# Sliding attention: the second product with the values stationary and the probabilities moving

## The reference, cut to what matters

```
sc = einsum('bcqhgd,bckhd->bchgqk', qb, kb) * HEAD_DIM ** -0.5      # kb, vb: the chunk before and the own chunk
sc = where(mask, sc, NEG_INF)
probs = softmax(concatenate([sc, sink], -1))[..., :-1]
o = einsum('bchgqk,bckhd->bcqhgd', probs, vb)                        # then reshape to (b, s, C_WIDTH)
mix = concatenate([y_a, y_b, y_c], -1) @ w_out[i]
```

## Time and profile before

| | |
|---|---|
| three runs, median (lowest to highest) | 1235.37 us (1234.68 to 1235.66) |
| profiled execution, span | 1233.0 us |
| its own time | not listed apart from the three runs |
| TensorE busy | 1226.3 us, 99% |
| VectorE busy | 839.8 us, 68% |
| ScalarE busy | 610.8 us, 50% |
| GpSimd busy | 136.2 us, 11% |
| TensorE's granted clock | 1.000 on average |

### The profile page before, as it was taken

How to read it: one execution, slowest core, us unless ns; L and a number is a source line. 1 busy time by engine, 2 the same in 40 slices (tenths; PEclk the granted TensorE clock), 3 DMA queues, 4 the chain that set the end, 5 groups by cost and what they waited for, 6 DMA issues and landing times.

```text
span 1233.0 us, 20630 instructions
## 1 busy us (share of the span) xinstructions
PE 1226.3 (99%) x8009; PEld 1128.1 (91%) x8009; DVE 839.8 (68%) x1365; ACT 610.8 (50%) x1156; POOL 136.2 (11%) x209
## 2 busy tenths in 40 slices
PE   9999999999999999999999999999999999999998
PEld 8999888999999998888899999889999999888887
DVE  5675545988888853268976746368888887433788
ACT  7444334555555642237664444264655555322474
POOL 2003531000000000003030036120000000000120
PEclk9999999999999999999999999999999999999999
DMA  7323232233333353320242222322333333444001
GB/s 251 104 65 90 70 103 69 69 102 105 104 103 103 103 188 142 131 69 18 86 122 68 90 65 69 103 77 67 114 104 103 104 103 121 154 154 171 18 18 69
DMA packets 124464, 122.32 MB, mean 99 GB/s; under 512 B 5200, under 2 KB 108752, under 8 KB 124368
## 3 DMA queue, kind: packets, MB, share of 16 engines
q1 hardware_dynamic: 123680, 120.48, 31.0%
q10 hardware_dynamic: 688, 0.53, 0.1%
HBM read 118.90 MB, written 2.10 MB: 98 GB/s over the span
## 4 chain that ended last, share of the span: by engine, by line
PE 98%; DVE 1%; ACT 0%; POOL 0%; issue 0%; DVEq 0%; ACTq 0%
PE bank L993 30%; PE bank L995 30%; PE bank L994 30%; PE bank L1203 2%; PE bank L1262 1%; PE bank L1285 1%; PE bank L1331 1%; PE bank L1283 1%; PE bank L1315 1%; PE bank L1270 0%; PE bank L1307 0%; PE bank L1327 0%; PE bank L1336 0%; PE bank L1213 0%; PE bank L1357 0%; PE bank L1244 0%
## 5 line engine op out<-in xcount | busy, mean ns | idle before, releaser
L993 PE MATMUL bank<-w_hi,h_hi 128*128 128x384 f32 (+2 forms) x564 | 201.2, 357 | 0.6 <-DVE w_lo L1892 0.5
L994 PE MATMUL bank<-w_lo,h_hi 128*128 128x384 f32 (+2 forms) x564 | 194.7, 345 | 0.0
L1890 DVE TENSOR_TENSOR w_lo<-raw,w_hi 128x1024 fp32r<-128x1024 f32 x70 | 83.7, 1234 | 133.7 <-ACT w_hi L1409 133.4
L993 PE MATMUL bank<-h_hi,w_hi 128*128 128x256 f32 x568 | 161.0, 284 | 0.1
L995 PE MATMUL bank<-h_hi,w_lo 128*128 128x256 f32 x568 | 160.7, 283 | 0.0
L994 PE MATMUL bank<-h_lo,w_hi 128*128 128x256 f32 x568 | 160.7, 283 | 0.0
L995 PE MATMUL bank<-w_hi,h_lo 128*128 128x384 f32 (+2 forms) x468 | 157.5, 337 | 0.0
L1409 ACT ACTIVATE w_hi<-raw 128x1024 fp32r<-128x1024 f32 x70 | 70.6, 1053 | 160.6 <-PE bank L995 160.6
L995 PE MATMUL bank<-w_hi,mid_lo 128*128 128x512 f32 x352 | 137.0, 389 | 0.0
L993 PE MATMUL bank<-T_hi,w_hi 128*128 128x256 f32 x448 | 126.8, 283 | 0.0
L994 PE MATMUL bank<-T_lo,w_hi 128*128 128x256 f32 x448 | 126.8, 283 | 0.0
(11 more groups left out here) (296 smaller groups left out, 2942.8 us busy)
## 6 DMA issues: line engine op xcount, KB each, us to landing
raw<-in_w_ffn_in SPq DMA_DIRECT2D x88, 512.0 KB, 3.9
raw<-in_w_ffn_out SPq DMA_DIRECT2D x44, 512.0 KB, 4.2
raw<-in_w_in SPq DMA_DIRECT2D x40, 384.0 KB, 3.8
raw<-in_w_out SPq DMA_DIRECT2D x16, 512.0 KB, 3.8
gw<-in_w_gate SPq DMA_DIRECT2D x16, 512.0 KB, 3.7
raw<-in_w_in SPq DMA_DIRECT2D x10, 512.0 KB, 4.1
raw<-in_w_ple SPq DMA_DIRECT2D x4, 512.0 KB, 6.3
x<-in_x_in SPq DMA_DIRECT2D x3, 512.0 KB, 6.9
```

Source lines behind the costliest of these rows:

```text
L993: pe.matmul(out_ap, a_hi, b_hi, start=start, stop=False, skip_group_check=True)
L994: pe.matmul(out_ap, a_hi, b_lo, start=False, stop=False, skip_group_check=True)
L1890: last = dve.tensor_tensor(lo, raw[q % RAWS][:, cols], hi, ALU.subtract)
```

## The change

The second product is turned round. Stationary are now the values (128 keys by 64 values of one group), moving are the transposed probabilities of the three heads of the group (384 columns). The result stands transposed in PSUM, group 0 on partitions 0 to 63 and group 1 on 64 to 127, so the transposes of `swa_yT` and their step are gone, and `y_hi` and `y_lo` are made at `swa_o`. As no ones column can give the sums any more, the exponentials write them (`accum_out`), and the probabilities are scaled before they are transposed, in a new step `swa_norm` on VectorE at u+4. The transposes move to u+5 and the product to u+7. The two heads that now share a row of 128 are one of each group, so the rows of `w_out` are put in that order before the launch.

```diff
-        for step, name in zip((0, 1, 4, 6, 8), ("swa_cur", "swa_prev", "swa_PT", "swa_o", "swa_yT")):
+        for step, name in zip((0, 1, 4, 5, 7), ("swa_cur", "swa_prev", "swa_norm", "swa_PT", "swa_o")):
...
-    swa_y = [place(f"swa_y{i}", [P, C_HEADS, HD], F32, (110, 48)[i]) for i in range(2)]
...
-    cv = place("cv", [P, TILES, 2, HD + 1], F32, 207.75)
-    dv = place("dv", [P, 2, 2, HD + 1], F32, 210)
+    cv = place("cv", [P, TILES, 2, HD], F32, 207.75)
+    dv = place("dv", [P, 2, 2, HD], F32, 210)
...
                 elif kind == "swa_PT":
                     c = e[1]
-                    pe.wait_ge(swa_exp, layer * TILES + c + 1)
+                    pe.wait_ge(swa_pn, layer * TILES + c + 1)
...
-                    for hh in range(C_HEADS):
-                        o = swa_bank(c, 0)[:, hh * (HD + 1):(hh + 1) * (HD + 1)]
-                        g = hh // 3
-                        if c:
-                            pe.matmul(o, ptu[c % 2][:, hh, :], cv[:, c - 1, g, :], start=True, stop=False,
-                                      skip_group_check=True)
-                        last = pe.matmul(o, ptl[c % 2][:, hh, :], dv[:, c % 2, g, :] if c else cv[:, 0, g, :],
-                                         start=(c == 0), stop=True, skip_group_check=True)
-                    last.then_inc(swa_o, 1)
-                elif kind == "swa_yT":
-                    c = e[1]
-                    pe.wait_ge(swa_yr, layer * TILES + c + 1)
-                    flat = swa_y[c % 2][:, :, :].rearrange("p h d -> p (h d)")
-                    for k in range(3):
-                        last = pe.transpose(swa_bank(c, 1)[:, k * P:(k + 1) * P], flat[:, k * P:(k + 1) * P],
-                                            T_("ident"))
+                    pairs = ([(ptu[c % 2], cv[:, c - 1, :, :]), (ptl[c % 2], dv[:, c % 2, :, :])] if c
+                             else [(ptl[0], cv[:, 0, :, :])])
+                    for i, (probs, values) in enumerate(pairs):
+                        for g in range(2):
+                            last = pe.matmul(swa_bank(c, 1)[rows(g), 0:BW], values[:, g, :],
+                                             probs[:, 3 * g:3 * g + 3, :], start=(i == 0),
+                                             stop=(i == len(pairs) - 1), skip_group_check=True)
                     last.then_inc(y_T, 1)
...
                     if c >= 2:
-                        act.wait_ge(y_T, y_count(layer, ("swa_yT", c - 2)))
+                        act.wait_ge(swa_PT, layer * TILES + c - 1)
...
                         act.activation(prob[c % 2][:, hh, :], prob[c % 2][:, hh, :], ACT.Exp, scale=HD ** -0.5,
-                                       bias=negm[c % 2][:, hh:hh + 1])
+                                       bias=negm[c % 2][:, hh:hh + 1], accum_out=psum_k[c % 2][:, hh:hh + 1])
...
                     if c > 2:
-                        pool.wait_ge(swa_o, layer * TILES + c - 1)
+                        pool.wait_ge(y_T, y_count(layer, ("swa_o", c - 2)))
...
+                elif kind == "swa_norm":
+                    c = e[1]
+                    o = c % 2
+                    dve.wait_ge(swa_exp, layer * TILES + c + 1)
+                    step(dve.tensor_tensor(rl[o], psum_k[o], esink[o], ALU.add))
+                    step(dve.reciprocal(rl[o], rl[o]))
+                    done(dve.tensor_tensor(prob[o][:], prob[o][:], rl[o][:, :, None].to_broadcast([P, 6, P]),
+                                           ALU.mult), swa_pn)
...
                 elif kind == "swa_o":
-                    c = e[1]
-                    o = c % 2
-                    dve.wait_ge(swa_exp, layer * TILES + c + 1)
-                    dve.wait_ge(swa_o, layer * TILES + c + 1)
-                    both = swa_bank(c, 0)[:, 0:6 * (HD + 1)].rearrange("p (h e) -> p h e", h=6)
-                    step(dve.tensor_tensor(rl[o], both[:, :, HD], esink[o], ALU.add))
-                    step(dve.reciprocal(rl[o], rl[o]))
-                    done(dve.tensor_tensor(swa_y[o][:], both[:, :, 0:HD],
-                                           rl[o][:, :, None].to_broadcast([P, 6, HD]), ALU.mult), swa_yr)
-                elif kind == "swa_yT":
                     c = e[1]
                     y_split(layer, e, swa_bank(c, 1)[:, 0:BW].rearrange("p (k t) -> p k t", k=3),
                             y_hi[:, 5:8, c * P:(c + 1) * P], y_lo[:, 5:8, c * P:(c + 1) * P])
...
+def heads_in_pairs(w):
+
+    low = AW + BW
+    c = w[:, low:].reshape(w.shape[0], C_KV, C_HEADS // C_KV, HD, D).transpose(0, 2, 1, 3, 4)
+    return np.concatenate([w[:, :low], c.reshape(w.shape[0], C_HEADS * HD, D)], 1)
```

More of the change, by code:

```diff
@@ L33 @@
 C_HEADS = 6
+C_KV = 2
 BW = B_HEADS * HD
@@ L514, in build_trunk @@
     esink = [small(6) for _ in range(2)]
+    psum_k = [small(6) for _ in range(2)]
     rl = [small(6) for _ in range(2)]
@@ L587, in build_trunk @@
     dv_ready = sem("dv_ready")
-    swa_o = sem("swa_o")
-    swa_yr = sem("swa_yr")
+    swa_pn = sem("swa_pn")
     ret_T = sem("ret_T")
@@ L665, in build_trunk @@
     for layer, e in schedule:
-        if e[0] in ("swa_yT", "ret_yT", "gmlp_yT"):
+        if e[0] in ("swa_o", "ret_yT", "gmlp_yT"):
             order_yT += [(layer, e)] * (2 if e[0] == "gmlp_yT" else 1)
@@ L1158, in block_of @@
                             pe.wait_ge(y_lo_ready, y_count(layer, ("ret_yT", 3)))
-                    need = {2: ("ret_yT", m), 3: ("swa_yT", m), 1: ("ret_yT", m), 0: ("gmlp_yT",)}[i]
+                    need = {2: ("ret_yT", m), 3: ("swa_o", m), 1: ("ret_yT", m), 0: ("gmlp_yT",)}[i]
                     if m == 3:
@@ L1255, in _ @@
                         if c >= 2:
-                            pe.wait_ge(y_lo_ready, y_count(layer, ("swa_yT", c - 2)))
+                            pe.wait_ge(y_lo_ready, y_count(layer, ("swa_o", c - 2)))
                     else:
@@ L1302, in _ @@
                     else:
-                        pe.wait_ge(y_lo_ready, y_count(layer, ("swa_yT", 2)))
+                        pe.wait_ge(y_lo_ready, y_count(layer, ("swa_o", 2)))
                     for i, src in enumerate((bk, bq)):
@@ L1343, in _ @@
                     if c == 0:
-                        pe.wait_ge(y_lo_ready, y_count(layer, ("swa_yT", 3)))
+                        pe.wait_ge(y_lo_ready, y_count(layer, ("swa_o", 3)))
                     elif c < TILES - 1:
@@ L1690, in _ @@
                                    ACT.Copy).then_inc(pt_copied0, 1)
-                elif kind == "swa_yT":
+                elif kind == "swa_o":
                     c = e[1]
@@ L1759, in _ @@
             pool.memset(neg_big, NEG).then_inc(pool_init, 1)
-            pool.memset(cv[:, :, :, HD:HD + 1], 1.0).then_inc(pool_init, 1)
-            pool.wait_ge(pool_init, 3)
+            pool.wait_ge(pool_init, 2)
             def pre(layer, stage, m):
@@ L1945, in _ @@
             dve.memset(still[:], 0.0).then_inc(still_zero, 1)
-            dve.wait_ge(pool_init, 3)
+            dve.wait_ge(pool_init, 2)
             spent = {}
@@ L2387 @@
         "bs_t": np.asarray(gmlp_bs).transpose(0, 2, 1),
-        "gn_w": np.asarray(ret_gn_w).reshape(depth, 3, P).transpose(0, 2, 1), "sinks": attn_sinks, "w_out": w_out, "post_mix": norm_mix_post,
+        "gn_w": np.asarray(ret_gn_w).reshape(depth, 3, P).transpose(0, 2, 1), "sinks": attn_sinks, "w_out": heads_in_pairs(np.asarray(w_out)), "post_mix": norm_mix_post,
         "w_ffn_in": w_ffn_in, "w_ffn_out": w_ffn_out, "post_ffn": norm_ffn_post,
```

## The result

The changed kernel takes 1250.39 us (median of 4 runs, 1249.01 to 1252.59), the kernel before 1235.24 us beside it. The ratio is 1.0125, with a 95% interval from 1.0112 to 1.0138: 15.2 us slower, where 12.0 were forecast. Slower, inside the range of 1240 to 1253, and 3.0 us above the predicted 1247.4. The share lost is small, but clear of the interval. Its four runs go from 1249.0 us at a mean granted clock of 0.996 to 1252.6 at 0.992.

The account below looks back on a forecast made before the run. TensorE was taken to bound the kernel, busy 1226.3 of 1233.0 us. Per layer, 9.7 us of waits against 3.7 saved gave 6.0, so +12.0 on the median 1235.37: 1247.4 us, range 1240 to 1253.

Parts of the forecast that it names:

- The mechanism: Before the probability transposes in attention: TensorE waits for VectorE's late scaling, 9.7 us of waits a layer.
- Waits in layer 0: TensorE before the transposes of chunks 0 to 3: 3.2, 1.0, 2.9 and 1.9 us.
- VectorE's signal of chunk 0: End of chunk 0's scaling at 59.7 us, with TensorE ready for the transposes at 56.55 us.
- The saving: TensorE's own attention work: 10.7 us removed and 6.95 added, so 3.7 us less a layer.
- the new product: Turned second product on TensorE: 1.9 us a chunk with change of shape, 1.25 in chunk 0.
- The 0.322 us for an instruction: New product on TensorE: each 384-column f32 instruction, scaled by columns from 0.215 for the gMLP product's 256.
- The factor of 0.68: New product's two column halves side by side on TensorE: time multiplied by 0.68, eight instructions in 1.75 us.
- The score product: Nearest row for overlapping halves on TensorE: 0.073 us per 128-column instruction where half of 0.215 would be 0.107.
- Rival 2: Same waits, but TensorE's clock falls after chunks 0 and 2 of both layers, 2 to 4 us each: 1253 to 1260; chance 0.12.
- The wait of chunk 3's scores: TensorE waits 0.7 us for ScalarE's late score copies, behind the 512-column split between norm and chunk 2's mask.
- The sums: On ScalarE, accumulator reads behind the six exponentials: 0.09 us each, 0.55 a chunk.
- The other side: Rival 3: VectorE keeps up, waits stay below 3.7 us a layer, faster, 1228.0 us with none; chance 0.08.

Follow-up runs that it names:

- e1: Changed kernel without the scaling of the probabilities and TensorE's wait for it (sum and reciprocal stay, output not normalized): 1233.1 us.
- e5: Changed kernel without the scaling (output not normalized), transposes and product back at their old places u+4 and u+6: 1226.5 us.
- e2: Changed kernel with the scaling at unit u+2 in place of u+4, same work: 1240.2 us.
- e7: Changed kernel with the scaling at u+1, right behind the maximum, and chunk 3 started at unit 29 in place of 28: 1230.1 us.
- e3: Changed kernel with the new product's loops exchanged, both products of group 0 and then both of group 1: 1250.7 us.
- e6: Changed kernel with 13 unused f32 products on TensorE ahead of the waits of chunks 0 and 2 in each layer: 1245.4 us.
- e10: Changed kernel with transposes and product one unit later (u+6, u+8), scaling left at u+4: 1229.4 us.
- e12: As e7, but with chunk 2's scaling one unit later (25): 1228.1 us, ratio 0.9942 to the kernel before.
- e8: As e7, but with the sums and the scaling done by GpSimd in place of VectorE: 1234.1 us.
- e4: Kernel before with only the scaling moved ahead (sums from exponentials, scaling u+4, transposes u+5, old product u+7, its transposes u+9): 1257.5 us.
- e9: As e7, but with chunk 2's product one unit later (31 in place of 30): 1235.0 us.
- e11: Changed kernel with scaling at u+1, transposes at u+6 and product at u+8, chunk 3 started at unit 28: 1237.8 us.

## Why the prediction was right, and where its sizes were off

- **The mechanism was right.** The transposes wait for the scaling, which stands behind a split and two rotary passes. Waits in layer 0: forecast 3.2, 1.0, 2.9, 1.9 us, measured 3.04, 1.26, 3.11, 1.15; in layer 1, which was taken to be the same, 3.06, 1.26, 3.47, 1.14. VectorE's signal of chunk 0 was forecast for 59.7; it comes at 59.37 + 0.96 = 60.33, in an execution in which the first scores start 0.64 us later (45.41, not 44.77). e1 and e5 show that the loss goes with the scaling, e2 and e7 that its place decides.
- **The saving was too small in the sum.** Forecast 3.7 us a layer, measured 5.0 (e5). The term at fault is the new product: 1.44 us for eight instructions, not 1.9, and 0.79 in chunk 0 (69.07 to 69.86), not 1.25. The 0.322 us for an instruction, scaled from 256 columns, was right: the pairs of `ptl` instructions start 0.33 us apart (e3). The factor of 0.68 for two halves at work side by side was not: eight instructions in 1.44 us are 0.18 each, and four of them take 0.70 (84.80 to 85.50), 0.175 each, a factor of 0.54. The score product was the wrong row to scale from; why it is slower is not shown. The 1.25 was also a slip of the sum, as 4 x 0.322 x 0.68 is 0.88 and the change of shape adds no more than 0.2. With the measured durations the prediction's sum gives 10.7 - 5.1 = 5.6 us saved a layer; the other 0.6 is not explained.
- **The clock was missing in the sum.** The prediction says itself that it is wrong if the clock drops behind the waits, and the clock did. Rival 2 had a chance of 0.12, and its condition came true in chunks 0 and 2 of layer 0 and in chunk 2 of layer 1. The work lost 1.7, 2.9 and 1.7 us by it, near the lower end of the 2 to 4 that the rival gave, and three times, not four. Its 1253 to 1260 was too dear for this, and because it put the clock on top without the larger saving.
- **So the nearness was luck.** 17.5 of waits + 6.3 of clock - 10.1 saved = 13.7, and 1.4 us of the 15.15 by which the two stretches grew stay open. The forecast of 12.0 came from 19.4 of waits - 7.4 saved. A saving too small by 2.7 us and waits too long by 1.9 stand against a clock left out at 6.3.
- **The wait of chunk 3's scores** (0.7 us in the walk) did not show in the changed kernel, as half the clock made TensorE arrive later. Where the clock stayed full it is there, at 0.36 us a layer (e6), and it set the time of e1 (2.6 us a layer).
- **The sums** cost what was taken: the six exponentials with their reads take 2.32 us (0.387 apart), where they took 1.77 before (49.26 to 51.03, where ScalarE's next operation starts), so 0.55 more, as forecast. The scaling took 0.96, as forecast.
- **The other side** needed waits below the saving. It did not come in this version, but e7, e10 and e12 show that it was two or three numbers of the plan away.
- **Open.** A layer's stretch without waits takes 124.5 - 0.7 = 123.8 us in e5. With its waits and its lost clock added, this meets e1 within 0.1 us (128.2 measured) and e12 within 0.3; it falls short by 0.4 in e10, by 0.5 and 0.8 in the changed kernel, by 1.0 and 0.7 in e8, and for e4, counted from the kernel before, by 1.3 a layer. No run was made for these. Why the clock fell behind some waits and not behind others of the same length is not settled either: chunk 0's wait in layer 1 of the changed kernel (3.06 us) is as long as in layer 0.

## What to carry to other kernels

When a step is moved in front of the busiest engine's next instruction, look up how late the engine that does it already is at that place, and what it has to finish first; its share over the whole span does not say this (68% here). A change can save on the engine that bounds the kernel and still lose: here 10.1 us saved came with 17.5 us of waits and some 6 of clock, and the same work in other places of the queue gained 7.2 us. Remove waits one at a time and look again, since each may cover the next, as e1, e9 and e11 show.

## What was not expected of the hardware

- The granted clock fell to half behind single waits in the middle of full work. Over the profiled executions of all kernels here it fell behind 14 of 17 waits of 2.6 to 3.7 us, behind 3 of 7 of 1.9 to 2.4 us (e2, e7 and e8), and behind none of 1.8 us or less. Each time the lower clock took 1.7 us, or twice that. Products on unused data in the wait kept it at 1.000 and were worth 5.0 us (e6).
- Two float32 products on the two halves of the array's columns overlap almost wholly, in either order of issue (e3): 0.175 us for each instruction of 384 columns, where one after the other they would take an estimated 0.322 (scaled from 0.215 for 256 columns). The Trainium skill, TensorEngine Tiling (Array Packing), section Theoretical Speedup, says up to twice as fast for a small dimension of up to 64; 0.322 against 0.175, a factor of 1.8, agrees with it.
- GpSimd at work slows VectorE: a split of 2.20 us took 3.42 beside GpSimd's scaling (e8).
- A power of six numbers for each partition takes GpSimd 1.3 us, nearly as long as a product of 768 (1.7 us).
